# Two mLSTM and attention mixers in a ten-stage kernel: gating, transposes and copies put elsewhere in four engine programs

## The reference

```python
def _mixer(h, w_in, w_out, ...):
    proj = (h @ w_in).astype(jnp.float32)
    da_q, da_k, da_v, ml_qk, ml_v, ml_o, ml_g = jnp.split(proj, SPLIT_IDX, axis=-1)
    y_da = _diff_attention(da_q, da_k, da_v, ...)      # 4 heads of 128: p0 - lam * p1, values, RMS norm
    y_ml = _mlstm(ml_qk, ml_v, ml_o, ml_g, ...)
    return jnp.concatenate([y_da, y_ml], axis=-1) @ w_out

def _mlstm(qk, v, o, gates, conv_w, conv_b, gate_b, norm_g):
    qk = jax.nn.silu(_causal_conv(qk, conv_w, conv_b))
    ...                                                # running sums of log gates, per head
    w = exp(D - m) * (q @ k.T)                         # decays times scores
    h = (w @ v + ...) / maximum(abs(den), exp(-m))
    h = _rmsnorm(h, norm_g).reshape(B, S, ML_WIDTH)
    return jax.nn.sigmoid(o) * h
```

## Time and profile before

| | |
|---|---|
| median of 3 executions | 2106.32 us (2106.2 to 2108.9) |
| profiled execution | 2108.29 us |
| its span, first to last instruction | 2106.4 us |
| mean granted TensorE clock | 0.982 |
| busy: TensorE, VectorE, ScalarE, GpSimd | 93%, 39%, 30%, 3% of the span |
| first mixer | about 1273 to 1400 us of the span |
| second mixer | about 508 us later |

### The profile page before, as it was taken

How to read it: one execution, slowest core, us unless ns; L and a number is a source line. 1 busy time by engine, 2 the same in 40 slices (tenths; PEclk the granted TensorE clock), 3 DMA queues, 4 the chain that set the end, 5 groups by cost and what they waited for, 6 DMA issues and landing times. The chain is left out here.

```text
span 2106.4 us, 38510 instructions
## 1 busy us (share of the span) xinstructions
PE 1964.7 (93%) x17260; PEld 1447.2 (69%) x17260; DVE 830.9 (39%) x1335; ACT 633.4 (30%) x1060; POOL 63.4 (3%) x103
## 2 busy tenths in 40 slices
PE   6999889897989999889889999999999999999998
PEld 5544344445775444444459988879988998878997
DVE  3111111114641111111156546875545554776552
ACT  2000000004430000000054436664435443665441
POOL 0000000000000000000020000010000000011000
PEclk8999999999999999999999999999999999999999
DMA  9999999997569999999966545336545555424551
GB/s 391 426 427 426 427 425 426 427 427 290 209 238 401 427 426 426 427 426 427 427 274 215 186 162 180 128 115 218 183 178 197 196 180 180 154 102 178 182 189 66
DMA packets 57058, 599.80 MB, mean 285 GB/s; under 512 B 6576, under 2 KB 6832, under 8 KB 9776
## 3 DMA queue, kind: packets, MB, share of 16 engines
q1 hardware_dynamic: 55728, 593.79, 70.9%
q10 hardware_dynamic: 1152, 3.41, 0.5%
HBM read 596.12 MB, written 1.05 MB: 284 GB/s over the span
## 5 line engine op out<-in xcount | busy, mean ns | idle before, releaser
L1860 DVE TENSOR_TENSOR SPLIT<-RING,SPLIT 128x2048 fp32r<-128x2048 f32 (+2 forms) x178 | 399.9, 2256 | 184.0 <-ACT SPLIT L1356 183.8
L671 PE MATMUL PS<-RING,WK 128*32 128x512 f32 x800 | 360.7, 605 | 49.9 <-DMA RING<-in_w_down 28.3
L528 PE MATMUL PS<-HTH,SPLIT 128*128 128x256 f32 x1344 | 383.9, 286 | 0.0
L530 PE MATMUL PS<-HTH,SPLIT 128*128 128x256 f32 x1344 | 380.3, 283 | 0.0
L529 PE MATMUL PS<-HTL,SPLIT 128*128 128x256 f32 x1344 | 380.3, 283 | 0.0
L1356 ACT ACTIVATE SPLIT<-RING 128x2048 fp32r<-128x2048 f32 (+2 forms) x178 | 333.4, 1887 | 78.3 <-DMA RING<-in_units 77.2
L671 PEld LDWEIGHTS PS<-RING,WK 128*32 128x32 f32 x800 | 85.2, 111 | 288.7 <-issue 254.8
L528 PEld LDWEIGHTS PS<-HTH,SPLIT 128*128 128x128 f32 x1344 | 257.8, 192 | 1.9 <-issue 1.3
L529 PEld LDWEIGHTS PS<-HTL,SPLIT 128*128 128x128 f32 x1344 | 257.9, 192 | 0.5
L530 PEld LDWEIGHTS PS<-HTH,SPLIT 128*128 128x128 f32 x1344 | 257.8, 192 | 0.0
L1498 ACT ACTIVATE WK<-PS 128x128 f32<-128x128 f32 x64 | 17.8, 278 | 710.4 <-PE PS L641 705.8
(11 more groups left out here) (323 smaller groups left out, 2086.8 us busy)
## 6 DMA issues: line engine op xcount, KB each, us to landing
RING<-in_units SPq DMA_DIRECT2D x171, 1024.0 KB, 4.8
RING<-in_w_up SPq DMA_DIRECT2D x54, 2048.0 KB, 37.2
RING<-in_w_down SPq DMA_DIRECT2D x52, 2048.0 KB, 34.5
RING<-in_w_gate SPq DMA_DIRECT2D x44, 2048.0 KB, 34.1
WK<-in_w_gate SPq DMA_DIRECT2D x20, 2048.0 KB, 34.6
WK<-in_w_up SPq DMA_DIRECT2D x10, 2048.0 KB, 37.6
WK<-in_w_down SPq DMA_DIRECT2D x10, 2048.0 KB, 32.5
RING<-in_units SPq DMA_DIRECT2D x4, 768.0 KB, 16.1
```

The lines of the kernel that those rows point to most:

```text
L528: pe.matmul(out, ll, rh, start=start, stop=False)
L530: return pe.matmul(out, lh, rh, start=False, stop=stop)
L671: t = pe.matmul(PS[32 * i:32 * i + 32, 4 + h, :], mo.HE[:, pb, 32 * f:32 * f + 32], v[:, c, 512 * h:512 * h + 512], start=f == 0, stop=f == 3)
L1860: dv.tensor_tensor(unit_part(u, 1), loaded(u), unit_part(u, 0).bitcast(F32), ALU.subtract).then_inc(s_lo, 1)
```

## The change

The program changes in both mixers of the second block:

- `close(b)` is split. A new `gated(z)` multiplies two heads of YM, both token blocks, by the sigmoid into a new place YS (the former DQ), one 128x512 instruction for each z, while GpSimd has still to make the norm factors. `close(b)` is then one 128x512 instruction, YS times the factors, in place of four.
- The transposes of a recurrence block go to two PSUM banks of half use each (6 and 7 for block 0, 4 and 5 for block 1) instead of one, and tell ScalarE after each two; VectorE's low halves follow after each two high halves.
- On TensorE `turn_recurrence(0)` is called inside out(0,1), ahead of its second six products, and decays(3) inside out(0,0) in the same way.
- On VectorE the first pair of attention low halves comes ahead of decayed(2) instead of behind it; gated(0) and gated(1) stand around sums(2) and sums(3).
- On ScalarE the copy of the transposed probabilities of head 2 comes ahead of the exponentials of head 3.

```diff
--- before.py
+++ after.py
@@ -372,6 +372,7 @@
         mx.R2 = al(256)
         mx.YD = al(1024).rearrange("p (b n) -> p b n", b=2)
         mx.YM = mx.QK.rearrange("p c n -> p (c n)")[:, 0:1024].rearrange("p (b n) -> p b n", b=2)
+        mx.YS = mx.DQ.rearrange("p h n -> p (h n)").rearrange("p (b n) -> p b n", b=2)
 
         mx.E = [mx.G4[:, 0:384], mx.G4[:, 512:896]]
         mx.SSD, mx.RSD, mx.SSM, mx.RSM = (SM[:, 80 + 8 * z:88 + 8 * z] for z in range(4))
@@ -1243,11 +1244,13 @@
 
             def turn_recurrence(b):
 
-                pe.wait_ge(s_ymn, 8 * l + 4 * b + 4)
-                pe.wait_ge(s_mem, 4 * l + 4)
+                pe.wait_ge(s_ymn, 2 * l + b + 1)
+                pe.wait_ge(*((s_ym, 4 * l + 4) if b else (s_mem, 4 * l + 4)))
                 for i in range(4):
-                    t = pe.transpose(PS[:, 6 + b, i * 128:i * 128 + 128], mx.YM[:, b, i * 128:i * 128 + 128], ident)
-                t.then_inc(s_yt, 1)
+                    t = pe.transpose(PS[:, 6 - 2 * b + i // 2, (i % 2) * 128:(i % 2) * 128 + 128],
+                                     mx.YM[:, b, i * 128:i * 128 + 128], ident)
+                    if i % 2:
+                        t.then_inc(s_yt, 1)
 
             def out(k, b, done=None, before=None):
 
@@ -1310,13 +1313,11 @@
             sums(1)
             turn_attention(0)
             turn_attention(1)
-            decays(3)
-            out(0, 0)
+            out(0, 0, before=lambda: decays(3))
             sums(2)
             sums(3)
             out(1, 0)
-            out(0, 1, s_unit)
-            turn_recurrence(0)
+            out(0, 1, s_unit, lambda: turn_recurrence(0))
             turn_recurrence(1)
             out(2, 0)
             out(3, 0, s_half)
@@ -1728,7 +1729,7 @@
                                (s_ysq, 8 * l + 2 * h + b + 1))
 
                 def attention_turned(z):
-                    ac.wait_ge(s_yt, 4 * l + z + 1)
+                    ac.wait_ge(s_yt, 6 * l + z + 1)
 
                     ac.wait_ge(s_unit, u0 + 11)
                     for i in range(2):
@@ -1737,9 +1738,10 @@
                                       scale=ve(f"yg{l}")[:, c:c + 1]).then_inc(s_oh, 1)
 
                 def recurrence_turned(b):
-                    ac.wait_ge(s_yt, 4 * l + 3 + b)
                     for i in range(4):
-                        ac.activation(HTH[:, b, 4 + i, :], PS[:, 6 + b, i * 128:i * 128 + 128], ACT.Copy,
+                        if i % 2 == 0:
+                            ac.wait_ge(s_yt, 6 * l + 2 + 2 * b + i // 2 + 1)
+                        ac.activation(HTH[:, b, 4 + i, :], PS[:, 6 - 2 * b + i // 2, (i % 2) * 128:(i % 2) * 128 + 128], ACT.Copy,
                                       scale=ve(f"yg{l}")[:, 4 + i:5 + i]).then_inc(s_oh, 1)
 
                 def decays(h):
@@ -1797,8 +1799,8 @@
                 column(1)
                 outs(1)
                 column(2)
+                weights(2)
                 scores(3)
-                weights(2)
                 probs(3)
                 column(3)
                 outs(2)
@@ -2420,9 +2422,9 @@
                                                 ALU.subtract).then_inc(s_ol, 1)
 
                 def recurrence_turned(b):
-                    dv.wait_ge(s_oh, 8 + 12 * l + 4 * b + 8)
                     for i in range(4):
-                        dv.scalar_tensor_tensor(HTL[:, b, 4 + i, :], PS[:, 6 + b, i * 128:i * 128 + 128],
+                        dv.wait_ge(s_oh, 8 + 12 * l + 4 + 4 * b + (i | 1) + 1)
+                        dv.scalar_tensor_tensor(HTL[:, b, 4 + i, :], PS[:, 6 - 2 * b + i // 2, (i % 2) * 128:(i % 2) * 128 + 128],
                                                 ve(f"yg{l}")[:, 4 + i:5 + i], HTH[:, b, 4 + i, :].bitcast(F32), ALU.mult,
                                                 ALU.subtract).then_inc(s_ol, 1)
 
@@ -2460,14 +2462,22 @@
                     dv.tensor_tensor(mx.YM[:, :, h * 128:h * 128 + 128], o[:, :, 0:128],
                                      dn.unsqueeze(2).to_broadcast([128, 2, 128]), ALU.mult).then_inc(s_ym, 1)
 
+                def gated(z):
+
+                    dv.wait_ge(s_so, 2 * l + 2)
+                    dv.wait_ge(s_ym, 4 * l + 2 * z + 2)
+                    a = 256 * z
+                    dv.tensor_tensor(mx.YS[:, :, a:a + 256], mx.YM[:, :, a:a + 256], mx.SO[:, :, a:a + 256],
+                                     ALU.mult).then_inc(own.up(), 1)
+
                 def close(b):
 
                     dv.wait_ge(s_nrs, 4 * l + 4)
-                    dv.wait_ge(s_so, 2 * l + b + 1)
-                    for h in range(4):
-                        y = mx.YM[:, b, h * 128:h * 128 + 128]
-                        dv.scalar_tensor_tensor(y, y, mx.RSM[:, 2 * h + b:2 * h + b + 1], mx.SO[:, b, h * 128:h * 128 + 128],
-                                                ALU.mult, ALU.mult).then_inc(s_ymn, 1)
+                    settle()
+                    rs = mx.RSM.rearrange("p (h b) -> p b h", b=2)[:, b, :]
+                    dv.tensor_tensor(mx.YM[:, b, :].rearrange("p (h n) -> p h n", h=4),
+                                     mx.YS[:, b, :].rearrange("p (h n) -> p h n", h=4),
+                                     rs.unsqueeze(2).to_broadcast([128, 4, 128]), ALU.mult).then_inc(s_ymn, 1)
                 lv = mx.LR.rearrange("p (a k n) -> p a k n", a=2, k=2)
                 dv.wait_ge(s_lam_in, 16 * l + 16)
                 dv.tensor_tensor(lv[:, :, 0, :], lv[:, :, 0, :], lv[:, :, 1, :], ALU.mult).then_inc(own.up(), 1)
@@ -2541,14 +2551,16 @@
                 attention_normed(1)
                 decays(2)
                 sums(1)
+                attention_turned(0)
                 decayed(2)
-                attention_turned(0)
                 attention_turned(1)
                 decays(3)
                 decayed(3)
                 lo(u0 + 14)
+                gated(0)
                 sums(2)
                 sums(3)
+                gated(1)
                 close(0)
                 close(1)
                 recurrence_turned(0)
```

## The result

The changed kernel took **2115.12 us** (median of 8, 2113.66 to 2117.21). The kernel before, run beside it and counted with its earlier runs, has 2108.92 us (median of 8, 2106.2 to 2112.46), 2.6 us more than the 2106.32 of its first three. The ratio is 1.003, 95% interval 1.0021 to 1.004: slower by 0.3%. The forecast was 2114.9 us, from a difference of 8.6 us on the old median; the measured difference is 6.2 us. So the closeness of the two totals is in part luck: the difference was too large by 2.4 us, and the base too small by 2.6, and the two errors cancel.

What follows compares the result with a forecast made beforehand. TensorE, busy 93% of the span, was taken as the bound. Per mixer 2.65 us plus 1.64 for the clock made 4.3, 8.6 in all, put on the median 2106.32 us: 2114.9 us, range 2108.5 to 2117.

Steps and rivals of the forecast that it cites:

- Step 1: ScalarE's copy ahead of head 3's exponentials: TensorE's 0.6 us wait goes, about 0.1 given back; -0.5 us per mixer.
- Step 2: VectorE's low halves around decayed(2): out(0,0) waits for all four anyway, so 0 won; it starts at 1372.7.
- Step 3: decays(3) inside out(0,0): TensorE's wait before it grows from 1.23 to 3.15 us; out(1,0) starts 1.25 us later.
- Step 4: Chain behind decays(3) on VectorE, ScalarE and GpSimd: starts 1376.5, sums end 1384.05, close(0) starts 1386.0, ends 1386.7.
- Step 5: Recurrence transposes inside out(0,1): TensorE waits 2.5 us for close(0); out(2,0) starts at 1389.35, +2.65 us per mixer so far.
- Step 6: TensorE's clock: a slow stretch behind the second wait as well as the first, +1.64 us per mixer, bounds 0 and 3.3.
- (b): Rival: the clock never falls in the mixers; +1.2 us per mixer, 2108.7 us; chance 0.10.
- (a): Rival: the clock stays up after the second wait in one or both mixers; 2111.6 to 2113.3 us; chance 0.30.
- (c): Rival: TensorE runs decays(3) while out(0,0) waits; -1.2 us per mixer, 2103.9 us, or down to 2097.2; chance 0.07.
- (d): Rival: shorter closing chain, second wait shrinks to 1 us without slow stretch; +1.15 us per mixer, 2108.6 us; chance 0.04.
- (e): Rival: a third slow stretch per mixer, as the long wait drags two behind it; 2118.2 us; chance 0.05.

Runs made afterwards that it cites:

- e5: The kernel before with only ScalarE's copy of head 2's probabilities moved ahead of scores(3); mixers 126.14 and 124.79 us, ratio to before 0.9998.
- e6: The kernel before with only VectorE's first attention low halves moved ahead of decayed(2); both mixers 126.87 us, ratio to before 1.0008.
- e2: The kernel before with only decays(3) moved inside out(0,0) on TensorE; mixers 130.12 and 127.93 us, ratio to before 1.0035.
- e1: The changed kernel with decays(3) back ahead of out(0,0) and decayed(2) back ahead of the low halves; mixers 125.41 and 125.11 us, ratio to before 0.9992.
- e10: e4 with lo(u0+14) moved ahead of decays(3) on VectorE; mixers 128.76 and 127.18 us, ratio to before 1.0014.
- e3: The kernel before with the recurrence part alone (gated(), short close(), two banks, transposes in out(0,1)); mixers 125.89 and 127.20 us, ratio to before 0.9997.
- e4: The changed kernel with 12 unread 512-column products filling TensorE's wait before out(0,0); mixers 129.60 and 130.82 us, ratio to before 1.0013.
- e12: e9 with turn_recurrence(0) behind out(0,1) again, two banks kept; mixers 123.12 and 124.78 us, ratio to before 0.9969.
- e11: e10 with gated(0) also moved, so both gated() stand behind sums(3); mixers 125.76 and 125.73 us, ratio to before 0.9997.
- e9: e1 with sums(2) ahead of out(0,0) on TensorE, and on VectorE sums(2) ahead of decayed(3), gated() behind sums(3); mixers 123.42 and 123.43 us, ratio 0.9985.

## Why the prediction was right, step by step

**Step 1, the copy: right.** -0.53 us in e5, -0.5 forecast. The expected part was given back: 0.29 us before L1178, for the SiLU.

**Step 2, the low halves: right as to the changed kernel.** out(0,0) started at 1373.30 - 0.48 = 1372.8 us, 1372.7 forecast. Alone, on the order of the kernel before, it costs 0.2 us (e6), where I had nothing.

**Step 3, decays(3) inside out(0,0): right.** The wait is 3.23 us, 3.15 forecast. e2 shows that this step alone makes the loss. The rest gains: the first mixer of e1, which has neither this order nor that of step 2, is 1.26 us shorter than before with the slow stretch in the same place. Of that, step 1 gives 0.53, and the wait of 1.07 us that went, less its new wait of 0.81, gives 0.26. The transposes give the other 0.5: before, all eight stood ahead of the wait and took 1.24 us; now each four hold up the next product by 0.39 and 0.36 us only (e1, 1388.65 to 1389.04 and 1390.52 to 1390.88).

**Step 4, the chain behind it: right but for its end.** Less the 0.48, VectorE's decays(3) started at 1376.4 (1376.5 forecast), lo ended at 1381.3 (1381.05), sums at 1384.2 (1384.05). gated(0) took 0.60 us to the next start (0.7). But close(0) started at 1386.6, not 1386.0: the pause of 1.97 us that I carried over from before was 2.5 us. GpSimd's power for head 2 took 1.23 us instead of 0.7, and head 3's two instructions stood behind it, as its rows show. I had called gated(1) hidden under the pause; it is what lengthened it, as far as the rows of all runs tell (see the last section). I had put the sigmoid down as still in time; that holds in the changed kernel, and no longer when lo is taken out of the chain (e10).

**Step 5, the second wait: its place and cause right, its size wrong,** 1.12 and 0.84 us for 2.5. TensorE came 2.1 us later than forecast (1387.89 - 1.12 - 0.48 = 1386.3 for 1384.2), mainly because two slow stretches lay ahead of that point instead of one. out(2,0) began at 1389.64, 1389.35 forecast. And the mixer is 2.70 us longer, for 2.65. Part of this closeness is luck: close(0) came 0.6 us late, and from the first transpose to out(2,0) it took 2.23 us where I had 2.6, since the transposes held TensorE for 0.75 us and not for 1.24.

**Step 6, the clock: the step that failed.** I added 1.64 us per mixer for a slow stretch behind the second wait. In the changed kernel there was none; one extra stretch (two in the second mixer) lay behind the first. A slow stretch ahead of the second wait is mostly absorbed by it, since VectorE sets that point: e1's mixers, one with and one without such a stretch, are 0.30 us apart, and their second waits 0.81 and 2.05 us. A stretch behind the second wait is paid: e3's mixers are 1.31 us apart, the stretch before the wait in one and behind it in the other. Adding 1.64 us for each stretch wherever it fell was the mistake. Worked out from e4, whose first mixer less its stretch is 127.96 us (rival (b) had 1.2 over the old 126.67), the two stretches of the changed kernel's first mixer cost 1.4 us together and the three of its second 2.3; this is an estimate, since e4 has the products of the filling besides. The Trainium skill (TensorE: Matmul & The Clock Gate, "What's actually happening") says that idleness brings the throttle back. I drew from it that a slow stretch would stand behind either wait, which is more than that sentence says; the trace has a slow stretch behind the first wait and none behind the second. The measured 6.33 us of the two mixers is the 2 x 2.65 of steps 1 to 5 and 1.0 more for the third stretch of the second mixer and small change, not 2 x 4.3. Rival (a), no slow stretch behind the second wait (2111.6 us, +5.3), describes the difference best; on the new base of 2108.92 it would have said 2114.2.

**The rivals.** (b) fell: the clock did fall in both mixers of the changed kernel. (c) fell: decays(3) began at 1375.21, behind the first six products, though VectorE had finished decayed(2), the last thing that decays(3) needs, by 1372.4, and TensorE stood until 1373.30. (d) is seen in part: the second wait did shrink to 1.1 us, by the slow stretches and not by a shorter chain, which came out longer. (e), a third stretch, came in the second mixer and cost under 1 us.

## What to carry to other kernels

A wait that another engine sets is a place with free room: before moving an instruction out of it, look for what else could stand there (here sums(2) did), and follow who on the other engines starts by the moved instruction, because their whole chain moves with it. Price a slower clock by where the next wait is: ahead of a wait that another engine ends it cost little here (0.30 us in e1, some 0.7 each by the estimate above where there were two or three), behind it nearly all (1.31 us more in e3). When one link is taken out of a chain, look at the second-longest beside it before writing down the gain. And before calling an instruction hidden in another engine's time, see whether that engine slows down beside it.

## What the runs showed of the hardware that I had not expected

The length of TensorE's wait does not tell whether the clock falls. The wait of 1.23 us before out(0,0) was followed by a slow stretch in both mixers of the kernel before and in the first mixers of e1, e3 and e5, but not in the second mixers of these three. 3.04 us was spared in the second mixer of e2, and 0.36 us was followed by one in the second mixer of e12 (1880.80 to 1884.21). The waits of e2 and e12 in their second mixers, and the clock behind e2's wait in the first mixer and in the second:

```profile
1884.72 0.47 PE L528 MATMUL PS<-SPLIT,HTL 128*128 128x512 f32 x1 [3.04 <-DVE HTL L2417]
```

```profile
1880.52 0.52 PE L529 MATMUL PS<-SPLIT,HTL 128*128 128x512 f32 x1 [0.36 <-issue]
```

```profile
1375.00:1381.00 6.00, 6.00 (x16) 4.28 (x15) 2.96 (x6) 2.89 (x4) 0.00 (x0) 0.50 0.00 0
1886.00:1892.00 6.00, 6.00 (x34) 4.91 (x33) 4.13 (x8) 2.89 (x4) 0.00 (x0) 1.00 0.01 3
```

The same program thus shows mixers 2.19 us apart in one execution (e2). Why the clock falls in one and not in the other these traces do not settle. With wide products in the wait it stayed at 1.00 behind out(0,0) in all six mixers (both of e4, e10 and e11); without them it fell there in 10 of the 14 mixers that waited over 1 us.

GpSimd's power of 128x2, with which it makes the norm factors of a head, took 0.70 to 0.76 us in most rows and 1.23 us in others (1384.78 above) with the same shape. The long ones go with VectorE. In both mixers of the changed kernel, e1, e3, e4 and e10 the power for head 2 took 1.23 or 1.24 us, and each time it started within 0.02 us of gated(1), a VectorE product of 128x512 with both operands in SBUF. In e11, where it began while the two gated() ran, it took 1.03 us. In e9 and e12, where the two gated() lie between the powers for heads 2 and 3, and in the kernels without gated() (before, e2, e5, e6) both took 0.70 us, in e9 also beside small VectorE instructions and one that reads PSUM. e11 differs from e10 by the place of gated(0) alone. No run moves gated(1) alone, but in all 24 mixers the time of this power goes with what gated() does beside it. The power in the kernel before, and both in e9 with VectorE's gated() between them:

```profile
1380.88 0.70 POOL L477 TENSOR_TENSOR SM<-SM,MH 128x2 f32<-128x2 f32 x1
```

```profile
1376.62 0.70 POOL L478 TENSOR_TENSOR SM<-SM,MH 128x2 f32<-128x2 f32 x1
...
1378.94 0.70 POOL L478 TENSOR_TENSOR SM<-SM,MH 128x2 f32<-128x2 f32 x1
```

```profile
1377.52 1.28 DVE L2471 TENSOR_TENSOR WK<-WK 128x512 f32<-128x512 f32 x2
```

With the long power the pause between sums(3) and close(0) was 2.5 us in place of 1.97, on the path to the second wait, so the other place of the two gated() may be part of what e9 gains.
